# Late expert rows through one-hot products at a layer's end, in a two-layer encoder with a mixture of experts

## Chip, cores and metric

One core of a Trainium2 chip runs the whole program in one launch. The metric is the device time of that launch in microseconds (us), the median of three runs. A profiled execution gives the trace.

## What is computed

Two token groups (256 and 512 tokens, D_MODEL 1024, float32) pass through two layers that share weights between the groups, and a final RMSNorm. Together they are 768 tokens, six tiles of 128. Of the reference only this matters here:

```python
for l in range(DEPTH):                                   # DEPTH = 2
    h = rms_norm(x, norm_mix_g[l])
    x = x + hybrid_mixer(h, ...)                         # four mixers, gates, w_out
    h = rms_norm(x, norm_ffn_g[l])
    x = x + hierarchical_moe(h, ...)                     # 16 experts, top-2 of one group of 4
return rms_norm(x, final_norm_g)

# hierarchical_moe: combine[token, expert] is the weight of a chosen expert, else 0
hid = silu(h @ w1[e]) * (h @ w3[e]) * combine[..., e]
out = sum_e hid_e @ w2[e]
```

## The kernel before

**Stages.** Each layer has a head, a mixer and a tail. The head makes the normed, transposed rows of the six tiles and their first projections. The tail holds the output product, the routing, the experts, and adds what they give to x. After the last layer a short head (layer == L) has the final norm and the stores of the outputs. Each engine runs a program of its own in written order, and semaphores tie them. Between two layers SyncE waits until four engines have raised `layer_over`, clears the layer's semaphores, and raises `cleared`, for which each engine waits in `next_layer` (GpSimd only after its first gathers).

**Experts.** The tokens that chose an expert are scattered into 128-row blocks in DRAM. A block is loaded, transposed on TensorE (`turn_in`), multiplied (`up`), gated, multiplied again (`down`), and its rows leave PSUM through `rows_out`: VectorE copies columns 0 to 511 and ScalarE 512 to 1023 into `y_sb`, and ScalarE issues the store. `ORDER` has the twelve experts whose number is not 3 modulo 4 first; the last of them, at position LOOP = 11, runs in a loop whose count depends on the data. Then come the four late experts 3, 7, 11 and 15, at positions 12 to 15 (END = 15). Early rows go back into `blocks`, late rows into `late_dram`, which has one row of zeros behind its 512 rows.

**Bringing rows back.** `gather` (GpSimd, two indirect DMAs a tile) fetches a token's two rows of `blocks`, and `combine` (VectorE, two operations of 128x1024 a tile) adds them to x with weights. They run beside the late experts: `combine` of tile 0 at position 12, of 2 at 13, of 3 and 4 at 14, of 1 behind the copy of 12, and of 5 behind the copy of 15. What came from a late expert comes by `gather_late`, one indirect DMA a tile through `late_slots`, at the start of the next head, and `add_late` (VectorE, 128x1024) adds it with the weight `w_late`. Since a token's two experts lie in one group, it has at most one late expert. `split_late` (VectorE, behind the copy of position 2) makes `late_slots` and `w_late`; a token with no late row points to the zeros.

**The head.** For tile t: ScalarE squares x (`head_square`), VectorE makes the variance, GpSimd its power -0.5 (`power`), VectorE scales (`scale`), TensorE transposes (`turn`), ScalarE evicts to hT (`evict`). `x_new` counts tiles whose x is complete; SyncE then stores that tile to DRAM. Tiles 0 and 3 are projected plainly (`tile`); tiles 1, 2 and 4, 5 go in pairs through seven smaller products (`pair`), which need sums of weight quarters (`weights_sum`) and of row quarters (`rows_sum`). Before, in layer 1 the four weight sums stand first on VectorE, then add_late(0), tile 0's variance and scale, and add_late(1) and (2). In the last head VectorE has, per tile, variance(t+1), scale(t), add_late(t+3).

**Times of an engine's order.** GpSimd in the head of layer 1 before: gathers of tiles 0 to 4, then power(0), the gather of tile 5, then the other powers. The first gather waits for all four late stores:

```python
if t == 0:
    pool.wait_ge(late_out, 16 * LATE * layer)
    pool.wait_ge(combined, TOP * T * layer)
```

Lines of the profile: L632 gather, L639 combine, L648 gather_late, L844 add_late, L848 and L959 variance and power, L866 scale, L701 the head's transposes, L725 `tile`, L742 `pair`, L873 weights_sum, L882 rows_sum, L2167 turn_in, L2175 up, L2210 down, L2303 the late stores, L2580 VectorE's copy in rows_out, L822 the first of the rope operations.

## Time and profile before

| | us |
|---|---|
| median of three runs | 1974.15 (1974.12 to 1975.18) |
| profiled execution, its own time | 1973.74 |
| its span in the trace | 1971.8 |
| TensorE busy | 1899.3 (96%) |
| VectorE, ScalarE, GpSimd busy | 1134.3, 477.5, 400.4 |
| DMA | 376.32 MB, mean 191 GB/s |

The span runs from the first to the last record of the trace; 1.9 us of the execution's time lie around it. Busy shares are means over stages with quite different limits. Times in rows count from the span's start.

### The profile page before, as it was taken

The numbers are of one execution on the slowest core, as the hardware profiler recorded it, in microseconds if no ns is written. First come the engines' busy times: TensorE is split into PE (matmuls) and PEld (weight loads), VectorE is DVE, ScalarE is ACT, GpSimd is POOL, SyncE is SP. The second block draws the span as 40 slices with busy tenths as digits, with TensorE's granted clock in tenths as the row PEclk, the third lists the DMA queues.
The fourth block names the chain that finished last, engine by engine and source line by source line (L and its number), as shares of the span: only waits on it lengthen the run. The fifth ranks groups of instructions, "written<-read, shape, count | busy, mean of one in ns | idle before, by whom it ended". The sixth has DMA issues, their size and how long they took to land.

```text
span 1971.8 us, 25238 instructions
## 1 busy us (share of the span) xinstructions
PE 1899.3 (96%) x9028; PEld 1251.7 (63%) x9028; DVE 1134.3 (58%) x2171; ACT 477.5 (24%) x1048; POOL 400.4 (20%) x310
## 2 busy tenths in 40 slices
PE   8999999999999999999699999999999999999993
PEld 5655658755665545888565556586566655468882
DVE  4788732644786866111667886436457778641126
ACT  3133313343221011111132333132432300111112
POOL 1322233122220012000324222421222200210013
PEclk9999999999999999999899999999999999999997
DMA  4555677422328405999832121122223392179996
GB/s 178 203 203 203 228 276 270 176 99 79 127 86 322 156 33 217 411 393 369 329 112 113 75 75 75 43 86 81 86 86 118 126 347 91 70 274 424 384 373 235
DMA packets 77915, 376.32 MB, mean 191 GB/s; under 512 B 6705, under 2 KB 15281, under 8 KB 64578
## 3 DMA queue, kind: packets, MB, share of 16 engines
q1 hardware_dynamic: 43154, 260.35, 34.3%
q10 hardware_dynamic: 26000, 82.90, 11.0%
q0 software_dynamic: 8640, 31.46, 4.2%
q8 instruction: 75, 1.23, 0.3%
q14 instruction: 46, 0.38, 0.1%
HBM read 262.44 MB, written 113.30 MB: 191 GB/s over the span
## 4 chain that ended last, share of the span: by engine, by line
PE 89%; DVE 4%; DMA 3%; ACT 1%; issue 1%; POOL 1%; ACTq 0%; DVEq 0%; SPq 0%; POOLq 0%
PE bank L1030 41%; PE bank L2175 11%; PE bank L2035 8%; PE bank L2060 5%; PE bank L2210 5%; PE bank L1043 3%; PE bank L1056 2%; PE bank L1083 2%; PE bank L1121 2%; PE bank L742 2%; PE bank L1095 1%; PE bank L2167 1%; PE bank L1220 1%; PE bank L725 1%; DMA blocks<-ring,slots 1%
## 5 line engine op out<-in xcount | busy, mean ns | idle before, releaser
L1030 PE MATMUL bank<-x,ring 128*128 128x384 f32 x1056 | 360.2, 489 | 2.3 <-issue 2.3
L1030 PE MATMUL bank<-hT,ring 128*128 128x384 f32 x1056 | 359.7, 490 | 0.1
L1030 PEld LDWEIGHTS bank<-x,ring 128*128 128x128 f32 x1056 | 195.0, 190 | 135.2 <-issue 12.5
L1030 PEld LDWEIGHTS bank<-hT,ring 128*128 128x128 f32 x1056 | 195.3, 190 | 133.0 <-issue 10.2
L1525 DVE SCALAR_TENSOR_TENSOR reg_a<-cvx,pp,reg_a 128x783 f32<-128x783 f32 x120 | 142.7, 1189 | 4.3
L1284 ACT ACTIVATE sums<-bank 128x384 f32<-128x384 f32 x132 | 64.9, 491 | 250.0 <-PE bank L1030 243.9
L2571 DVE SCALAR_TENSOR_TENSOR prob<-prob,bank 128x256 f32<-128x256 f32 x30 | 12.6, 421 | 180.8 <-ACT prob L2290 180.7
L1468 DVE SCALAR_TENSOR_TENSOR gbuf<-bank,sums 128x384 f32<-128x384 f32 x96 | 53.5, 557 | 88.0 <-PE bank L1030 82.1
L1805 POOL TENSOR_TENSOR ring<-dg,ring 128x512 f32<-128x512 f32 x24 | 34.1, 1421 | 257.1 <-PE bank L1030 257.1
L2258 ACT ACTIVATE prob<-x 128x1024 f32<-128x1024 f32 x12 | 12.7, 1058 | 291.7 <-DVE x L2423 291.7
L2035 PE MATMUL bank<-oT,wide 128*128 128x384 f32 x256 | 82.9, 486 | 0.0
L2035 PE MATMUL bank<-oT,reg_a 128*128 128x384 f32 x256 | 82.9, 486 | 0.0
L1779 POOL TENSOR_TENSOR ring<-ring 128x512 f32<-128x512 f32 x44 | 60.6, 1378 | 99.0 <-PE bank L1030 76.6
L1298 ACT ACTIVATE gbuf<-gbuf,small 128x384 f32<-128x384 f32 x96 | 59.1, 615 | 74.2 <-DVE gbuf L1468 67.1
L1805 POOL TENSOR_TENSOR ring<-cvx,ring 128x512 f32<-128x512 f32 x20 | 25.4, 1272 | 242.9 <-PE bank L1030 242.9
L2367 POOL TENSOR_TENSOR small<-small 128x1 f32<-128x1 f32 x12 | 6.8, 564 | 315.1 <-DVE small L2428 315.1
L2035 PEld LDWEIGHTS bank<-oT,reg_a 128*128 128x128 f32 x256 | 48.6, 190 | 33.9
L2035 PEld LDWEIGHTS bank<-oT,wide 128*128 128x128 f32 x256 | 48.6, 190 | 33.9
L1030 PE MATMUL bank<-x,dg 128*128 128x384 f32 x192 | 65.9, 486 | 0.0
L2060 PE MATMUL bank<-hT,oT 128*128 128x512 f32 x144 | 65.7, 595 | 0.0
L1333 ACT ACTIVATE probT<-bank 128x256 f32<-128x256 f32 (+2 forms) x96 | 42.9, 446 | 92.2 <-PE bank L1095 89.2
L632 POOL DMA_INDIRECT ring<-blocks,slots x4 | 3.9, 964 | 301.0 <-SPq L2021 300.4
(387 smaller groups left out, 3276.2 us busy)
## 6 DMA issues: line engine op xcount, KB each, us to landing
ring<-in_wd SPq DMA_DIRECT2D x26, 2048.0 KB, 9.2
blocks<-hT SPq DMA_DIRECT2D x16, 3072.0 KB, 22.1
gate_dram<-gbuf ACTq DMA_DIRECT2D x64, 384.0 KB, 2.3
ring<-gate_dram SPq DMA_DIRECT2D x16, 1536.0 KB, 7.3
ring<-in_we SPq DMA_DIRECT2D x8, 2048.0 KB, 15.0
hT<-blocks ACTq DMA_DIRECT2D x26, 512.0 KB, 9.3
wide<-in_we SPq DMA_DIRECT2D x6, 2048.0 KB, 23.1
oT<-in_we SPq DMA_DIRECT2D x6, 2048.0 KB, 21.4
```

Source lines behind the costliest of these rows:

```text
L1030: mm = nc.tensor.matmul(bank[i % 2][:, 0:HALF], w[:, k, :], a[:, k, :], start=(k == 0 and r in (0, 1, 3)), stop=(k == 3), skip_group_check ...
L1043: mm = nc.tensor.matmul(bank[i % 2][:, 0:BW], a[:, k, p * P:(p + 1) * P], w[:, k, :], start=(k == 0 and r in (0, 1, 3)), stop=(k == 3), sk ...
L1284: out(activate(sums[:, r // 2 if r < 3 else 0, :], b, ACT.Copy, scale=scale), i)
L1298: done(activate(c, c, ACT.Tanh, scale=0.5, bias=half(n)), cv_tanh if name == "cv" else None)
L1468: ins = stt(to, b, scale, held_rows, ALU.mult, ALU.add)
L1525: done(stt(y, src, w, y, ALU.mult, ALU.add), last)
L1779: done(tensor_(b12, b12, b11, ALU.subtract), t_done)
L1805: done(tensor_(b11, t2_of(name, g), b11, ALU.subtract), t_done)
L2035: mm = nc.tensor.matmul(branch_bank(q)[:, 0:HALF], wb_sb[m // 4][:, n, k, (m % 4) * P:(m % 4 + 1) * P], oT[:, 2 * n + k, half[hf]], start= ...
L2060: mm = nc.tensor.matmul(bank[out_bank[r]][:, :], a[:, k, p * P:(p + 1) * P], w[:, k, :], start=(k == 0 and r not in (2, 5)), stop=(k == 3) ...
L2175: mm = nc.tensor.matmul(bank[s][:, j * P:(j + 1) * P], up_w[slot][:, k, j * P:(j + 1) * P], xT[s][:, k, :], start=(k == 0), stop=(k == KD ...
L2210: mm = nc.tensor.matmul(y_bank(b)[c][:, :], hidT[s][:, k, :], down_w[slot][:, k, c * 512:(c + 1) * 512], start=(k == 0), stop=(k == 1))
```

## The change

Tiles 0 and 1 (`BY_PRODUCT = 2`) no longer get the rows of the last two late experts (positions 14 and 15) by a gather. `split_late` makes for each of these tiles and each of the two experts a matrix of 128x128 that has, for each token with a row there, w_late at that row's column, and it turns such tokens' `late_slots` to the row of zeros. TensorE transposes the four matrices ahead of down(14), ScalarE evicts them into `sums`, and behind down(15) TensorE multiplies them with the two `y_sb` tiles into PSUM banks 4 to 7 (`end_product`). `add_end` (VectorE, two operations of 128x512 a tile) adds that to x. The gathers of tiles 0 and 1 fetch rows of the first two late experts alone: they are issued in the tail, behind the last `gather`, once those two stores have landed. Their places are now those of tile 2's early rows. combine of tile 5 moves from the tail's end to the next head: in layer 1 behind scale(2), in the last head behind scale(0) and add_end(1). In layer 1's head the weight sums stand behind it, the fourth one behind norm(3), and add_late(3), (4), (5) and the squares of tiles 3 and 4 have new places. TensorE raises `layer_over` behind the first end product. The last 256 rows of `late_dram` are set to zero once, in layer 0. Some semaphores are merged to make room for the new ones.

```diff
-                for t in range(3):
-                    if t == 2:
-                        variance(0)
-                    add_late(t)
-                for t in range(T):
+                combine(dve, L - 1, T - 1)
+                for t in range(1, T):
                     if t + 1 < T:
-                        variance(t + 1)
+                        add_late(t + 1)
+                    variance(t)
                     scale(t)
-                    if t + 3 < T:
-                        add_late(t + 3)
                 return
```

```diff
 def head_vector(dve, layer):
+            def add_end(t):
+                dve.wait_ge(end_mm, BY_PRODUCT * (layer - 1) + t + 1)
+                for c in range(2):
+                    xs = x[:, t, c * 512:(c + 1) * 512]
+                    done(tt(xs, end_bank[t][c][:, :], xs, ALU.add), x_new if c else None)
...
+            if layer:
+                add_late(0)
+                add_end(0)
+                add_late(1)
+                variance(0)
+                scale(0)
+                add_end(1)
...
             if layer:
-                for n in range(4):
-                    weights_sum(n)
-                add_late(0)
-                variance(0)
-                scale(0)
-                add_late(1)
                 add_late(2)
+                norm(1)
+                norm(2)
+                combine(dve, layer - 1, T - 1)
...
+            weights_sum(0)
+            weights_sum(1)
             rows_sum(1, 0)
             rows_sum(1, 1)
+            if layer:
+                add_late(3)
             pair(1, 1)
...
+            weights_sum(2)
+            rows_sum(1, 2)
+            if layer == 0:
+                weights_sum(3)
+            rows_sum(1, 3)
             norm(3)
+            if layer:
+                weights_sum(3)
             pair(1, 4)
             pair(1, 5)
+            if layer:
+                add_late(4)
+                add_late(5)
...
 def head_gpsimd(pool, layer):
-            for t in range(T - 1):
-                gather_late(pool, layer, t)
+            gather_late(pool, layer, 2)
+            gather_late(pool, layer, 3)
             pool.wait_ge(cleared, layer)
             pool.sem_inc(entered, 1)
-            power(0)
-            gather_late(pool, layer, T - 1)
-            for t in range(1, T):
+            for t in range(T):
                 power(t)
+                if t == 0:
+                    gather_late(pool, layer, 4)
+                if t == (1 if layer == L else 2):
+                    gather_late(pool, layer, 5)
...
 def head_scalar(act, layer):
             evict(2)
             head_square(act, layer, 3)
-            head_square(act, layer, 4)
+            if layer == 0:
+                head_square(act, layer, 4)
             for r in (0, 2, 3):
                 pair(1, r)
             evict(3)
             pair(1, 6)
+            if layer:
+                head_square(act, layer, 4)
             head_square(act, layer, 5)
...
 def tail_tensor(pe):
+                    elif b + 1 < NE:
+                        pe.wait_ge(table_done, 3)
+                        for n in range(2 * BY_PRODUCT):
+                            mm = nc.tensor.transpose(bank[2][:, n * P:(n + 1) * P], at_end[n // 2][n % 2], ident)
+                        mm.then_inc(xt_mm, 1)
                     down(b)
+
+                def end_product(t, n):
+                    for c in range(2):
+                        mm = nc.tensor.matmul(end_bank[t][c][:, :], end_rows[t][n], y_sb[n][:, c * 512:(c + 1) * 512],
+                                              start=n == 0, stop=n == 1)
+                    return mm
+
+                pe.wait_ge(xt_ev, pos(END) + 3)
+                pe.wait_ge(y_ev, pos(END))
+                pe.wait_ge(y_ev_act, pos(END))
+                end_product(0, 0)
+                pe.wait_ge(y_ev, pos(END) + 1)
+                pe.wait_ge(y_ev_act, pos(END) + 1)
+                pe.sem_inc(layer_over, 1)
+                end_product(0, 1).then_inc(end_mm, 1)
+                end_product(1, 0)
+                end_product(1, 1).then_inc(end_mm, 1)
...
 def tail_gpsimd(pool):
                     gather(pool, layer, t)
+                for t in range(BY_PRODUCT):
+                    gather_late(pool, layer + 1, t)
...
 def split_late():
+                    for t in range(BY_PRODUCT):
+                        for n in range(2):
+                            done(ts_(at_end[t][n], slot_no, end_slot[:, n, t:t + 1], w_late[:, t:t + 1], ALU.is_equal, ALU.mult),
+                                 table_done if t and n else None)
...
 def tail_vector(dve):
-                    for t in {LOOP + 1: (1,), LOOP + 3: (4,), LOOP + 4: (5,)}.get(b, ()):
+                    for t in {LOOP + 1: (1,), LOOP + 3: (4,)}.get(b, ()):
                         combine(dve, layer, t)
```

## Rows read from the trace of the kernel before

**Rows 1.** The page: busy us, share of the span and instructions of each engine.

```profile
PE 1899.3 (96%) x9028; PEld 1251.7 (63%) x9028; DVE 1134.3 (58%) x2171; ACT 477.5 (24%) x1048; POOL 400.4 (20%) x310
```

**Rows 2.** Windows: stretch, length, busy us of PE, PEld, DVE, ACT, POOL; PEclk, DMA.

```profile
969.20:983.80 14.60, 0.00 (x0) 0.00 (x0) 10.96 (x12) 1.69 (x3) 8.36 (x7) 0.66 0.60 208
...
1943.20:1943.40 0.20, 0.00 (x0) 0.00 (x0) 0.20 (x1) 0.00 (x0) 0.00 (x0) 0.63 0.90 369
```

**Rows 3.** Timeline from layer 0's end: start us, us, instruction [idle before <-releaser].

```profile
965.51 3.60 PE L2210 MATMUL bank<-reg_a,prob 128*128 128x512 f32 x8
...
969.35 0.69 DVE L2580 COPY hT<-bank 128x512 f32<-128x512 f32 x1
...
971.27 1.28 DVE L639 SCALAR_TENSOR_TENSOR x<-gbuf,small,x 128x1024 f32<-128x1024 f32 x1
973.02 1.23 DVE L873 TENSOR_TENSOR wide<-ring 128x1024 f32<-128x1024 f32 x1 [0.46 <-SPq L2642]
973.31 1.74 POOL L648 DMA_INDIRECT reg_b<-late_dram,late_slots  x1 [15.56 <-DMA late_dram<-hT]
...
979.01 1.28 DVE L844 SCALAR_TENSOR_TENSOR x<-reg_b,small,x 128x1024 f32<-128x1024 f32 x1 [0.98 <-DMA reg_b<-late_dram,late_slots]
...
981.58 0.15 DVE L848 TENSOR_SCALAR small<-small 128x1 f32<-128x1 f32 x1 [1.29 <-ACT prob L759]
981.82 0.57 POOL L959 TENSOR_TENSOR small<-small 128x1 f32<-128x1 f32 x1 [0.72 <-DVE small L848]
982.42 1.29 DVE L866 SCALAR_TENSOR_TENSOR reg_a<-x,small,probT 128x1024 f32<-128x1024 f32 x1 [0.69 <-POOL small L959]
...
983.86 1.94 PE L701 MATMUL bank<-consts,reg_a 128*128 128x128 f32 x8 [14.76 <-DVE reg_a L866]
...
986.58 7.55 PE L725 MATMUL bank<-ring,hT 128*128 128x512 f32 x12 [0.78 <-ACT hT L770]
```

**Rows 4.** Timeline of layer 1's head, further on.

```profile
993.96 1.04 PE L701 MATMUL bank<-consts,reg_a 128*128 128x128 f32 x8
...
998.80 0.69 DVE L882 TENSOR_TENSOR x<-hT 128x512 f32<-128x512 f32 x1 [3.85 <-ACT hT L770]
...
1001.41 5.42 PE L742 MATMUL bank<-wide,x 128*128 128x256 f32 x24 [0.36 <-ACT sums L782]
...
1011.81 1.36 DVE L822 TENSOR_TENSOR oT<-reg_b 128x1152 f32<-128x1152 f32 x1 [1.86 <-ACT reg_b L782]
...
1016.95 1.09 PE L701 MATMUL bank<-consts,reg_a 128*128 128x128 f32 x8 [0.65 <-DVE reg_a L866]
```

**Rows 5.** Timeline of the last head.

```profile
1945.18 0.94 POOL L648 DMA_INDIRECT reg_b<-late_dram,late_slots  x1 [14.66 <-DMA late_dram<-hT]
...
1949.82 1.28 DVE L844 SCALAR_TENSOR_TENSOR x<-reg_b,small,x 128x1024 f32<-128x1024 f32 x1 [5.40 <-DMA reg_b<-late_dram,late_slots]
...
1952.75 1.29 DVE L844 SCALAR_TENSOR_TENSOR x<-reg_b,small,x 128x1024 f32<-128x1024 f32 x1 [1.64 <-DMA reg_b<-late_dram,late_slots]
...
1954.31 1.54 POOL L959 TENSOR_TENSOR small<-small 128x1 f32<-128x1 f32 x1 [2.39 <-DVE small L848]
...
1968.71 0.33 SPq L2622 DMA_DIRECT2D y_sample<-hT  x1
```

**Rows 6.** One late store (956.1), one gather (956.8), and their times to landing.

```profile
L2303 ACTq DMA_DIRECT2D late_dram<-hT x1: 333/333/333, 956.1 to 956.1; - x1
...
DMA to landing us min/median/max: 5.3/5.3/5.3
...
L632 POOL DMA_INDIRECT gbuf<-blocks,slots x1: 937/937/937, 956.8 to 956.8; - x1
...
DMA to landing us min/median/max: 11.8/11.8/11.8
```

**Rows 7.** Groups by shape, 1600 to 1740 us; and timeline behind layer 0's split_late.

```profile
L2423 DVE SCALAR_TENSOR_TENSOR x<-bank,x 128x512 f32<-128x512 f32 x26 | 17.9, 690 | 11.3 <-PE bank L2060 10.9
...
835.39 0.42 DVE L2571 SCALAR_TENSOR_TENSOR prob<-prob,bank 128x256 f32<-128x256 f32 x1 [4.34 <-ACT prob L2290]
```

More of the change, by code:

```diff
@@ L116 @@
 FROM_BLOCKS = T - 2
+BY_PRODUCT = 2
 ML_UNITS = [(hp, p) for hp in range(HEADS // 2) for p in range(T // 2)]
@@ L547, in program @@
         setup_done, stored = once("setup_done"), once("stored")
-        late_out, combined = once("late_out"), once("combined")
+        late_out, end_out, end_mm = [once(f"late_out{n}") for n in range(2)], once("end_out"), once("end_mm")
+        combined = once("combined")
         layer_over, cleared, entered = once("layer_over"), once("cleared"), once("entered")
-        x_in, ident_in, consts_done = [once(f"x_in{t}") for t in range(T)], once("ident_in"), once("consts_in")
+        x_in, ident_in = [once(f"x_in{t}") for t in range(T)], once("ident_in")
         first_half, gain_spread = once("first_half"), once("gain_spread")
@@ L624, in y_late @@
         def y_late(t):
-            return reg_b[:, t * D:(t + 1) * D]
+            return reg_b[:, t * D:(t + 1) * D] if t >= BY_PRODUCT else back_place[2][t]
+        end_rows = [[sums[:, :, :].rearrange("p s c -> p (s c)")[:, (2 * t + n) * P:(2 * t + n + 1) * P] for n in range(2)]
+                    for t in range(BY_PRODUCT)]
+        end_bank = [bank[4:6], bank[6:8]]
         def gather(pool, layer, t):
@@ L643, in gather_late @@
         def gather_late(pool, layer, t):
-            if t == 0:
-                pool.wait_ge(late_out, 16 * LATE * layer)
-                pool.wait_ge(combined, TOP * T * layer)
+            if t < BY_PRODUCT:
+                pool.wait_ge(late_out[0], 16 * (2 * layer - 1))
+                pool.wait_ge(combined, TOP * (T * (layer - 1) + 3))
+            else:
+                pool.wait_ge(late_out[0], 32 * layer)
+                pool.wait_ge(end_out, 16 * layer)
+                pool.wait_ge(combined, TOP * (T * (layer - 1) + t + 1))
+            pool.wait_ge(late_out[1], 16 * layer)
             pool.indirect_dma_start(
@@ L768, in evict @@
                 act.wait_ge(ht_mm, t + 1)
+                if layer and t == 0:
+                    act.wait_ge(end_out, 16 * layer)
+                    act.wait_ge(late_out[0], 32 * layer)
                 for q in range(2):
@@ L1854, in mix_sync @@
                 sp.dma_start(late_dram[LATE * P:LATE * P + 1, :], zeros_in[0:1, :]).then_inc(zeros_out, 16)
+                for n in range(LATE - 2, LATE):
+                    sp.dma_start(late_dram[n * P:(n + 1) * P, :], zeros_in).then_inc(zeros_out, 16)
             sp.wait_ge(proj_mm, last_proj[MIX_CHUNKS - 2] + 1)
@@ L1924, in tail @@
             at_late, in_late = (part(752 + 48 * n, T * TOP * LATE).rearrange("p (a g) -> p a g", g=LATE) for n in range(2))
+            end_slot = part(872, 2 * BY_PRODUCT).rearrange("p (n t) -> p n t", n=2)
+            past_two, to_zero = part(880, BY_PRODUCT), part(888, BY_PRODUCT)
+            at_end = [[part((2 * t + n) * P, P) for n in range(2)] for t in range(BY_PRODUCT)]
             w_in, row_late = part(848, T * TOP).rearrange("p (t c) -> p t c", c=TOP), part(864, T)
@@ L1935, in y_free @@
                     eng.wait_ge(loop_over, 1)
-                elif b > LOOP + 2:
-                    eng.wait_ge(late_out, 16 * LATE * layer + 32)
+                elif b == LOOP + 3:
+                    eng.wait_ge(late_out[0], 16 * (2 * layer + 1))
+                elif b == END:
+                    eng.wait_ge(late_out[1], 16 * (layer + 1))
             start_f, expert_f, block_f = part(704, SPARE), part(720, SPARE + 2), part(736, SPARE + 1)
@@ L2302, in rows_out @@
                         n = b - LOOP - 1
-                        act.dma_start(late_dram[n * P:(n + 1) * P, :], y_sb[s]).then_inc(late_out, 16)
+                        act.dma_start(late_dram[n * P:(n + 1) * P, :], y_sb[s]).then_inc(end_out if b == END else late_out[n % 2], 16)
                 turn_in(0)
@@ L2345, in tail_scalar @@
                         turn_in(b + 2)
+                    elif b + 1 < NE:
+                        act.wait_ge(xt_mm, pos(END) + 2)
+                        activate(sums[:, :, :].rearrange("p s c -> p (s c)")[:, 0:4 * P], bank[2][:, :], ACT.Copy).then_inc(xt_ev, 1)
                     rows_out(b)
@@ L2363, in tail_gpsimd @@
                 pool.wait_ge(rows_init, 16 * NE)
-                pool.wait_ge(zeros_out, 16 * (layer + 2))
+                pool.wait_ge(zeros_out, 16 * (layer + 4))
                 for n, t in enumerate(tile_order):
@@ L2566, in split_late @@
                     done(tt(w_both, w_both, w_in, ALU.subtract))
+                    for t in range(BY_PRODUCT):
+                        for n in range(2):
+                            done(ts_(at_end[t][n], slot_no, end_slot[:, n, t:t + 1], w_late[:, t:t + 1], ALU.is_equal, ALU.mult),
+                                 table_done if t and n else None)
                 def hidden(b):
```

52 lines of the change are left out of this document (23 added, 29 removed).

## The prediction

> **What bounds the kernel.** I read the page first: TensorE is busy for 96% of the span [rows 1], so time can only be won where it stands still. The windows show the widest hole: from 969.20 to 983.80 us it does nothing at all [rows 2], and the same place comes once more at the end, after which it has no work left. Both are layer ends. Then I read the timeline across them.
>
> At layer 0's end the last down product starts at 965.51 and ends at 969.11. The rows go to DRAM, and VectorE combines tile 5 until 972.55. The gather of late rows starts on GpSimd at 973.31 and lands 5.6 us after that; VectorE, which had waited for it, adds tile 0 at 979.01 [rows 3]. So x of tile 0 is new at 980.30 (call such a moment X), the square, the power on GpSimd and the scaling follow, and TensorE gets its first transpose at 983.86. The reader is to see a chain of latencies in which each engine waits for the last.
>
> Behind it lies the head of layer 1. TensorE's tile products run on, and its wait ends last on VectorE again at 1016.95, for the scaled rows of tile 4 [rows 4]. From X to there before: 36.65 us. After 1016.95 its waits are of a kind that I take to move along unchanged. The last end is another thing: there the end is set by VectorE and GpSimd, x(0) is new at 1951.10 (1949.82 + 1.28), but VectorE is nearly full from 1952.75 on, and the last store goes at 1968.71, behind the last scaling [rows 5].
>
> **Start of the head, both ends.** Added to TensorE before the last but one down product: four 128x128 transposes. Eight take 1.04 us [rows 4], so 0.5 us, and nothing hides them: down(END) starts at 966.03 and ends at 969.63. ScalarE's extra eviction of 128x512 (0.6 us) falls in the time of the down product. VectorE's copy of the last rows started at 969.35 behind combine(4) and ended at 970.04 [rows 3]; now it ends near 970.36, the store goes 0.3 us later, and the first gather behind it (tile 2 now) starts at 973.64.
>
> The products: one down product is eight instructions of 128x512 in 3.60 us [rows 3], of which each end_product has four, 1.73 us. The first needs only the rows of the expert before the last, and follows at 969.5; the second needs the copy of 970.36, which is there, and runs 971.2 to 973.1. The other two hold TensorE until 976.6, when it has nothing else to do anyway. The clear of semaphores waits for TensorE's release behind the first product (about 971), then 0.47 us as now (972.55 to 973.02 [rows 3]), so add_late(0) of 1.28 us runs from 971.4 to 972.8 and is hidden. Its gather leaves GpSimd when the write of expert LOOP+2 has landed (956.1 + 5.3 = 961.4 [rows 6]), near 962. Then add_end(0): two operations of 128x512 from PSUM, 0.69 us each [rows 7] and 0.04 between: X = 974.53, 5.77 us earlier. All the same at the second end, 971.87 us later by the gathers' starts [rows 3, 5]: X = 1946.40 against 1951.10.
>
> **GpSimd.** power(0) is now queued behind two gathers that wait for the last store: tile 2 from 973.64 to 974.6, tile 3 from 974.9. A gather needs 0.94 us (1945.18 [rows 5]), but one that starts under a VectorE operation with both inputs in SBUF ends about 0.8 us after that operation: the gather of 973.31 took 1.74 us beside the subtraction of 973.02, which lasts 1.23 [rows 3]. add_late(1) runs 974.56 to 975.84, so tile 3's gather ends at 976.68, power(0) starts 0.2 later instead of at 976.05, and the scaling is 0.83 us late. I take that at both ends. The bounds are 0 and 1.3 (one such operation).
>
> The Trainium skill ("SBUF — State Buffer", Who interferes with whom) says that a VectorE operation with two SBUF inputs holds up only GpSimd's reads, and infers that descriptor generation goes free beside a tensor_tensor. The gather just named speaks against the inference. By that rule the 0.83 would fall away twice and the sum below be 1.7 us lower.
>
> **Head of layer 1, from X to the transpose of tile 4.** By VectorE's order: square 1.28, power 0.84, scale 1.29 as in [rows 3] (3.41); transpose at full clock and evictions until the square of tile 1, 2.25; its variance 1.25, power and scale 2.1 (9.0); the same for tile 2, 2.15 (11.2). Then the moved combine(5), 2.6, and two weight sums of 1.26, which before lay in the wait for gathers: 16.3. rows_sum twice, 0.73 each: 17.8. In before VectorE waited 3.85 us ahead of the row sums [rows 4]; that idle swallows most of the addition. add_late(3), 1.3: 19.1. Now the new wait: ScalarE has the square of tile 3 ahead of the eviction of pair(1,0), 1.1, so TensorE's pair(1,2) starts at 20.7 after a stall of some 2.9 us, where before it was 0.36 [rows 4]. VectorE: pair, weight sum, two row sums, variance and scale of tile 3: 26.0; weight sum and pair(1,4): 27.7; pair(1,5), bound by TensorE: 29.3; add_late(4) and (5), 2.6: 31.95; rope piece 0, 3.0 (two operations of 1.36, the first that of 1011.81 [rows 4], and a short one); variance and scale 2.1: 37.05; TensorE 37.1. That is 0.45 longer than the 36.65 of before, from an X that counts 5.77 - 0.83 = 4.94 earlier: a gain of 4.5 us.
>
> **Last head.** From X: scale(0) ends at 4.24 (with the 0.83); add_end(1) 1.45; combine(5) 2.6 that before lay in the wait for the gather: 8.3. Per tile then add_late 1.31, variance, power and scale 2.14. Before, variance(t+1) stood ahead of scale(t), so the power was hidden; now scale(t) stands right behind variance(t) and waits 0.66 of it each time. Four such tiles of 3.45 and a last of 2.15: X + 24.25 = 1970.65. The last store then goes at 1970.7, against 1968.71: a loss of 2.0 us.
>
> **The clock.** The granted clock is at its upper level (2.4 GHz) until the idle of 14.6 us and then at the lower, and the transposes and the first twelve instructions of tile 0 take 1.94 and 7.55 us against 1.04 and 5.2 at full clock (twelve at the pace of the down product's eight) [rows 3, 4]. Now TensorE is idle for only 2.4 us before the first transpose, and 2.9 before pair(1,2). At the last end it fell 2.3 us behind the last product (1940.98 to 1943.3), at layer 0's end after about 4.7 (a mean of 0.66 over 14.6 us between 1.0 and 0.5) [rows 2], so either gap may or may not cost it. Bounds: 0, and 3.2 (0.9 + 2.3, what it costs now). I take 0.7, since VectorE's chain hides the rest.
>
> **Hidden at no cost.** split_late gets six small operations (0.2 us) and four one-hot ones of 128x128 (under 0.35 us each, half of 128x512), 2.6 us on VectorE, which idled 4.34 behind it [rows 7]; uncovered, they would cost 2.6 twice. Two more stores of zeros stand in SP's queue in layer 0, among the mixer's products, where nobody waits for SP. The merged semaphores change no order. SP's x stores and the load of the next chunk move with x(3), from 992.5 to about 995.5; it is used after 1017.
>
> **Sum.** -4.5 + 2.0 + 0.7 = -1.8 us. The profiled execution took 1973.74 (span 1971.8 and 1.9 around it), so 1971.9; the median of the runs is 0.4 higher: 1972.4.
>
> **Rivals.** *Faster*: GpSimd isn't held and the clock stays up: 0.83 twice and 0.7 better, -4.2, 1970.0. For it: the skill's rule, and add_end reads PSUM. Against: the rows of 973.31 and 1954.31, where a power of 0.57 took 1.54 beside VectorE [rows 5]. Chance 0.22. Beyond it lies a head bound by TensorE alone, 1968.
>
> *Slower*: the work put on VectorE is not swallowed in layer 1's head. combine(5) 2.6, four weight sums 5.0 and add_end(1) 1.45 are 9.1 (the 0.45 found above counts them with the idle they fill); if all of it is on the path, the head loses 4.1, and with 2.0 and 0.7 the time is 1981. It decides against the change once less than 2.9 of the 9.1 finds a gap. Against it are the 3.85 and 1.86 us of idle in [rows 4]. Chance 0.1.
>
> *It does not do what it says*: the early gathers land late, since transfers are dense there. A gather issued at 956.8 took 11.8 us [rows 6]. From 962 and 963 that gives 973.8 and 975; X moves to 976.5, of which 1.2 count at the first end: 1973.6. Chance 0.15.
>
> **Numbers.** My forecast has 0.5, and 0.03 lies elsewhere. 0.2% is 3.9 us, about what a measurement can tell from no change. Faster by more than that needs the first rival or luck: 0.25. Slower: 0.12. Between: 0.63. The forecast's own range is 1970.5 to 1974.5; the range that holds 8 in 10 is 1968.0 to 1976.5.
>
> **What would show it.** In the profile after: first transpose of layer 1 near 978.9; a gather of 1.7 us ahead of power(0); TensorE idle 2 to 3 us before pair(1,2), ended by ScalarE; the transpose of tile 4 near 1012.5; in the last head waits of 0.66 us before each scale and the last store near 1967 on the new span's scale. Wrong it would be if the clock stays low for long, or add_late(0) waits for its gather.

## The result, and the profile after

The changed kernel took 1977.92 us (median of 14 runs, 1976.53 to 1982.79) where before took 1975.62 beside it: a ratio of 1.0015, 95% interval 1.0008 to 1.0022. A second set of runs of the same text gave 1978.05 against 1974.98, 1.0017 (1.0008 to 1.0026). So it is slower by 2.3 to 3.1 us by the medians, and by 3.0 and 3.4 by the ratios, which are taken without a few executions of 2036 us and more in the later sets. That is less than the 0.2% named above, but it lies outside the predicted range, and on its other side. The profiled execution took 1980.01 us, with a span of 1978.2.

The timeline of the changed kernel across layer 0's end and the start of layer 1's head answers to [rows 3] (start us, us, instruction, [idle before <-releaser]):

```profile
972.43 7.03 PE L2296 MATMUL bank<-hT,sums 128*128 128x512 f32 x16
...
973.40 0.33 ACTq L2361 DMA_DIRECT2D late_dram<-hT  x1
974.18 1.28 DVE L861 SCALAR_TENSOR_TENSOR x<-dg,small,x 128x1024 f32<-128x1024 f32 x1 [0.81 <-SPq L2716]
976.14 1.42 DVE L868 TENSOR_TENSOR x<-bank,x 128x512 f32<-128x512 f32 x2 [0.67 <-PE bank L2296]
...
977.59 1.28 DVE L861 SCALAR_TENSOR_TENSOR x<-reg_a,small,x 128x1024 f32<-128x1024 f32 x1
977.84 1.84 POOL L659 DMA_INDIRECT reg_b<-late_dram,late_slots  x1 [9.22 <-DMA late_dram<-hT]
...
979.99 0.94 POOL L659 DMA_INDIRECT reg_b<-late_dram,late_slots  x1 [0.30 <-issue]
980.96 0.57 POOL L986 TENSOR_TENSOR small<-small 128x1 f32<-128x1 f32 x1
981.56 1.28 DVE L890 SCALAR_TENSOR_TENSOR reg_a<-x,small,probT 128x1024 f32<-128x1024 f32 x1 [2.50 <-POOL small L986]
...
982.99 1.94 PE L712 MATMUL bank<-consts,reg_a 128*128 128x128 f32 x8 [3.54 <-DVE reg_a L890]
...
985.71 6.87 PE L736 MATMUL bank<-ring,hT 128*128 128x512 f32 x12 [0.78 <-ACT hT L784]
```

The end products do what was wanted: VectorE adds them at 976.14, and x of tile 0 is new at 977.56 with no gather behind the last store. But GpSimd's next gather (tile 2) waits for that store until 977.84, a second one follows, and only then comes power(0): VectorE stands idle for 2.50 us before the scaling, and TensorE for 3.54.

Further on in the same head, to the transpose of tile 4, which answers to [rows 4]:

```profile
996.09 1.09 ACT L784 ACTIVATE hT<-bank 128x512 f32<-128x512 f32 x2 [0.27 <-PE bank L712]
...
997.99 0.69 DVE L906 TENSOR_TENSOR x<-x,hT 128x512 f32<-128x512 f32 x1
998.71 1.28 DVE L861 SCALAR_TENSOR_TENSOR x<-reg_b,small,x 128x1024 f32<-128x1024 f32 x1
1000.03 1.06 ACT L770 ACTIVATE prob<-x 128x1024 f32<-128x1024 f32 x1 [2.86 <-DVE x L861]
...
1001.09 0.36 ACT L796 ACTIVATE sums<-bank 128x256 f32<-128x256 f32 x1
...
1001.60 3.02 PE L753 MATMUL bank<-wide,x 128*128 128x256 f32 x8 [2.09 <-ACT sums L796]
...
1019.64 1.09 PE L712 MATMUL bank<-consts,reg_a 128*128 128x128 f32 x8 [1.46 <-DVE reg_a L890]
```

TensorE stalls for 2.09 us ahead of 1001.60: ScalarE's eviction stands behind the square of tile 3, the square behind add_late(3), and that behind rows_sum. (Among the squares only that of tile 4 has a new place on ScalarE; the square of tile 3 stands where it stood before, and what moved is the addition that it waits for.)

The windows (length, busy us of PE, PEld, DVE, ACT, POOL; PEclk; DMA share; GB/s) show that both idle times cost the clock, as [rows 2] show it for the one of before:

```profile
979.46:982.99 3.53, 0.00 (x0) 0.03 (x1) 1.39 (x2) 0.00 (x0) 3.01 (x4) 0.84 0.69 216
983.00:988.00 5.00, 4.22 (x11) 2.71 (x12) 2.70 (x4) 2.94 (x5) 1.25 (x2) 0.50 0.85 260
999.50:1001.60 2.10, 0.01 (x2) 0.04 (x1) 0.52 (x2) 1.42 (x3) 0.00 (x0) 1.00 0.35 140
...
1003.00:1005.00 2.00, 2.00 (x6) 1.55 (x6) 1.80 (x4) 0.29 (x1) 0.01 (x1) 0.50 0.92 328
```

0.50 is the lower level (1.2 GHz), 1.00 the upper.

The last head, which answers to [rows 5] (two of the five tiles behind tile 0, and the last scaling):

```profile
1949.25 1.79 POOL L659 DMA_INDIRECT reg_b<-late_dram,late_slots  x1 [7.96 <-DMA late_dram<-hT]
...
1952.91 1.28 DVE L890 SCALAR_TENSOR_TENSOR hT<-x,small,probT 128x1024 f32<-128x1024 f32 x1 [2.50 <-POOL small L986]
...
1961.80 1.28 DVE L861 SCALAR_TENSOR_TENSOR x<-reg_b,small,x 128x1024 f32<-128x1024 f32 x1
...
1963.12 0.15 DVE L872 TENSOR_SCALAR small<-small 128x1 f32<-128x1 f32 x1
1963.36 0.56 POOL L986 TENSOR_TENSOR small<-small 128x1 f32<-128x1 f32 x1 [0.74 <-DVE small L872]
1963.95 1.28 DVE L890 SCALAR_TENSOR_TENSOR hT<-x,small,probT 128x1024 f32<-128x1024 f32 x1 [0.68 <-POOL small L986]
...
1967.41 1.28 DVE L890 SCALAR_TENSOR_TENSOR hT<-x,small,probT 128x1024 f32<-128x1024 f32 x1 [0.66 <-POOL small L986]
...
1973.00 1.29 DVE L890 SCALAR_TENSOR_TENSOR hT<-x,small,probT 128x1024 f32<-128x1024 f32 x1 [0.66 <-POOL small L986]
```

A tile takes 3.46 us (1963.95 to 1967.41), of which 0.66 is the wait for the power.

**The span added up.** From the end of each layer's last up product (before: 961.96 and 1933.83, after: 965.01 and 1936.36), the two spans, 1971.8 and 1978.2, divide like this: up to layer 0's end +3.0; from there to the transpose of tile 4 54.99 before and 54.63 after, -0.4; the body of layer 1 -0.2; from its last up product to the last store 34.88 and 37.95, +3.1; from that store to the end of the span 3.1 and 3.9, +0.8. Together +6.4 with rounding. The first +3.0 can't be called the change's: in the eleven further profiles below, all with the change's operations in layer 0, that point lies anywhere from 961.7 to 964.4, on average 0.7 behind the one profile of before, and a0_again, the same text, has it at 963.1. So some tenths of a us in layer 0 may be the change's; one profile of before can't tell. What is left, +3.3, is the cost at the two layer ends and behind them in this execution.

### The profile page after: what moved, and what is told of

Same layout as the page of the kernel before. It is cut to its first block, busy times and chain, and to the rows that moved or that the text cites. A ratio compares the mean times of both kernels' runs of the same rounds, so it can differ in the third digit from the quotient of the medians.

```text
span 1978.2 us, 25377 instructions
## 1 busy us (share of the span) xinstructions
PE 1915.3 (97%) x9068; PEld 1259.2 (64%) x9068; DVE 1144.6 (58%) x2199; ACT 478.9 (24%) x1050; POOL 399.6 (20%) x310
## 3 DMA queue, kind: packets, MB, share of 16 engines
q8 instruction: 75, 1.23, 0.2%
## 4 chain that ended last, share of the span: by engine, by line
PE 89%; DVE 4%; issue 2%; DMA 2%; POOL 1%; ACT 1%; ACTq 0%; POOLq 0%; DVEq 0%; SPq 0%
PE bank L1059 41%; PE bank L2211 10%; PE bank L2071 8%; PE bank L2096 5%; PE bank L2246 5%; PE bank L1072 3%; PE bank L1085 2%; PE bank L1112 2%; PE bank L1150 2%; PE bank L753 2%; PE bank L1124 1%; PE bank L2203 1%; PE bank L1249 1%; PE bank L736 1%; DMA blocks<-ring,slots 1%
```

## The experiments

All are compared by two stretches. A is the start of the last but one down product, which follows the four added transposes (some 0.45 us per layer end, so not in the stretches). The head stretch runs from A in layer 0 to the first transpose of tile 4; the end stretch from A in layer 1 to the end of the span. Between the two lies the body of layer 1, which is in neither: 917.3 us in the changed kernel, and from 916.8 to 921.7 in the others, so a difference of spans or of single times can't be put down to the two stretches alone. One execution each, and each ratio is to runs of before made beside that kernel's; the columns between say when scale(0) started in layer 1's head (from A), how long TensorE had stood idle before the first transpose and before pair(1,2), and whether the clock fell there.

| kernel | scale(0) | idle, first transpose | idle, pair(1,2) | head stretch | end stretch | ratio to before (95%) |
|---|---|---|---|---|---|---|
| before | 20.35 | 14.76, fell | 0.36 | 54.88 | 37.86 | 1 |
| changed | 16.00 | 3.54, fell | 2.09, fell | 54.08 | 41.29 | 1.0015 (1.0008 to 1.0022) |
| a0_again | 14.76 | 2.29, fell | 2.09, stayed | 51.86 | 41.32 | 1.0017 (1.0008 to 1.0026) |
| e1_power_first | 14.19 | 1.73, stayed | 4.47, fell | 54.30 | 41.17 | 1.0016 (1.0007 to 1.0025) |
| e4_pe_busy | 16.01 | 0.96, stayed | 1.23, stayed | 51.04 | 41.26 | 1.0012 (1.0003 to 1.0021) |
| e5_no_early_gathers | 14.77 | 2.30, stayed | 2.96, fell | 51.17 | 39.71 | 1.0010 (1.0002 to 1.0019) |
| e2_combine_tail | 16.29 | 3.83, fell | 2.09, fell | 54.62 | 38.66 | 1.0005 (0.9996 to 1.0014) |
| e3_var_early | 18.10 | 5.64, fell | 2.09, fell | 56.82 | 38.98 | 1.0003 (0.9994 to 1.0012) |
| e6_square3_later | 16.34 | 3.87, fell | none, stayed | 52.04 | 41.52 | 0.9994 (0.9985 to 1.0003) |
| e8_first_end_only | 16.00 | 3.54, fell | 2.09, stayed | 53.11 | 37.53 | 0.9993 (0.9984 to 1.0002) |
| e9_first_end_add3 | 17.54 | 5.07, fell | none, stayed | 53.04 | 37.72 | 0.9977 (0.9967 to 0.9988) |
| e10_both_new_order | 15.73 | 3.26, fell | none, stayed | 50.84 | 34.71 | 0.9972 (0.9960 to 0.9983) |
| e12_new_order_pe_busy | 16.30 | 1.26, stayed | none, stayed | 48.49 | 35.56 | 0.9969 (0.9956 to 0.9981) |

**a0_again: the changed kernel once more.**

> The changed kernel once more, beside the others, as their yardstick. Two stretches are read in each trace: the head stretch, from the end of layer 0's last up product to the first transpose of layer 1's tile 4 (before 54.99 us, changed 54.63), and the end stretch, from the end of layer 1's last up product to the issue of the last store (before 34.88, changed 37.95). All theories: 54.6 and 38.0 again, within 1 us.

The same text gave a head stretch 2.2 us shorter, where no more than 1 us of difference was expected. Its second moved gather had landed, at 971.4, when the last late store was issued at 971.5, and the store took 2.6 us; in the first profile that gather landed at 975.0, 1.6 us behind the store's issue, and the store took 3.7. So the gather of tile 2 could start at A + 11.21, where the first profile had 12.28, and it took 0.94 us and not 1.84; scale(0) came 1.24 us earlier and the clock fell once, not twice. The last end is the same to 0.03; there the gather of tile 2 started at A + 12.55. So one profile's head stretch of this kernel can't be read to better than 2 us unless it is said what the clock and the store did in it.

**e1_power_first: power(0) ahead of the two gathers.**

```
             pool.wait_ge(cleared, layer)
             pool.sem_inc(entered, 1)
             for t in range(T):
                 power(t)
                 if t == 0:
+                    gather_late(pool, layer, 2)
+                    gather_late(pool, layer, 3)
                     gather_late(pool, layer, 4)
```

> GpSimd takes power(0) of tile 0 ahead of the gathers of tiles 2 and 3. Theory Q (the late last store and the two gathers queued ahead of power(0) hold up the scaling of tile 0 by 1.9 us at both ends): the scaling starts 2.1 us after x of tile 0 is new instead of 4.0, head stretch 1 to 2 us shorter, end stretch 1.9 shorter, time 2 to 4 us less. Rival V (VectorE's longer list decides whatever GpSimd does, and gathers issued later make add_late(2) wait): under 1 us in each stretch.

The two gathers are taken out ahead of it. The scaling came 1.8 us earlier and the first clock loss was gone, but nothing was won: the gather of tile 2 now left at A + 14.36, add_late(2) waited 3.37 us for it, scale(1) came at 22.44 as in the changed kernel (22.46), and the stall before pair(1,2) grew to 4.47 us and took the clock there. At the last end it went the same way: scale(0) at 14.20, add_late(2) 1.79 us in wait, scale(1) at 23.52 for 23.57. The wait moved from power(0) to the gather, and the 2 to 4 us of the theory didn't come; the rival was right.

**e4_pe_busy: TensorE kept busy in both gaps** by products of 128x512 that nobody reads.

```
                 end_product(1, 1).then_inc(end_mm, 1)
+                if layer == 0:
+                    for n in range(3):
+                        nc.tensor.matmul(bank[3][:, :], end_rows[0][0], y_sb[0][:, 0:512], start=True, stop=True)
...
+                if layer and t == 1 and r == 2:
+                    for n in range(2):
+                        nc.tensor.matmul(bank[5][:, :], hT[:, 0, 0:P], w[:, 0, :], start=True, stop=True)
```

> TensorE gets idle work whose result nobody reads: three 128x512 products into a free bank behind layer 0's end products, and two ahead of pair(1,2), sized to lie inside the idle of 3.5 and 2.1 us. Theory C (the idle lets the granted clock fall twice, and that costs up to 3 us of the head stretch): clock at its upper level throughout, first transposes 1.04 us instead of 1.94, the 24 instructions of pair(1,2) to (1,4) 5.4 instead of 7.1, head stretch 1.5 to 3 us shorter, end stretch unchanged. Rival V (VectorE decides): clock up, head stretch the same within 0.5 us.

This is the clean measurement of the clock: scale(0) stands at 16.01, the first transpose at A + 17.44, as in the changed kernel's profile (16.00, 17.43), and the head stretch is 3.04 us shorter: pair(1,2) started 1.50 us earlier (34.54 for 36.04 from A) and took 1.7 less. The times show less of it: 1.0012 against 1.0015 and 1.0017, with intervals that overlap. In this execution the body of layer 1 took 919.25 us against 917.27, and no run says why. The windows of this kernel show the clock at its upper level in the gap, through the transposes and ahead of pair(1,2):

```profile
976.50:979.50 3.00, 3.00 (x8) 1.14 (x6) 0.46 (x3) 0.03 (x1) 2.52 (x4) 1.00 0.65 224
980.80:982.60 1.80, 1.05 (x8) 0.82 (x8) 1.73 (x3) 0.71 (x2) 0.70 (x1) 1.00 0.72 234
996.50:998.50 2.00, 0.77 (x4) 0.59 (x4) 0.59 (x2) 1.25 (x3) 0.00 (x0) 1.00 0.70 250
```

**e5_no_early_gathers: without the moved gathers of tiles 0 and 1.** The rows that they bring are missing, so x of tiles 0 and 1 lacks the earlier late experts.

```
-            dve.wait_ge(gathered[t], 16 * ((TOP + 1) * layer + TOP))
+            dve.wait_ge(gathered[t], 16 * ((TOP + (t >= BY_PRODUCT)) * layer + TOP))
...
-                dve.wait_ge(gathered[t], 16 * (TOP + 1) * layer)
+                if t >= BY_PRODUCT:
+                    dve.wait_ge(gathered[t], 16 * (TOP + 1) * layer)
...
-                for t in range(BY_PRODUCT):
-                    gather_late(pool, layer + 1, t)
```

> The two gathers of late rows for tiles 0 and 1 are left out, at both layer ends (add_late(0) and (1) still run, on what lies there). Theory D (these two transfers, now issued beside the last two late stores, make the last one land 1.2 us later): the last late store lands in 2.6 us instead of 3.7, the gather of tile 2 and power(0) come 1.1 us sooner, each stretch about 1 us shorter. Rival: the store is late because TensorE and VectorE are busy with its rows, so 3.7 us again and no gain.

The last store landed undelayed at both ends (the gather of tile 2 at A + 11.21 and 11.22; before had 11.24 at both), scale(0) stood at 14.77 at both, and the end stretch was 1.6 us shorter. Its timeline:

```profile
974.04 0.94 POOL L659 DMA_INDIRECT reg_b<-late_dram,late_slots  x1 [14.43 <-DMA late_dram<-hT]
...
975.28 1.69 POOL L659 DMA_INDIRECT reg_b<-late_dram,late_slots  x1 [0.30 <-issue]
...
976.98 0.58 POOL L987 TENSOR_TENSOR small<-small 128x1 f32<-128x1 f32 x1
977.60 1.28 DVE L891 SCALAR_TENSOR_TENSOR reg_a<-x,small,probT 128x1024 f32<-128x1024 f32 x1 [1.26 <-POOL small L987]
```

VectorE's wait for the power is 1.26 here, 2.50 in the changed kernel. The moved gathers thus cost about 1.2 us at an end where they are still on their way when the last store is issued; at a0_again's first end they weren't, and scale(0) stood at 14.76 with them. The head stretch is 2.9 us shorter than the changed kernel's, not 1, since the first clock loss went too: TensorE was idle for 2.30 us and kept its level.

**e2_combine_tail: combine(5) back behind the last copy.**

```
-                combine(dve, L - 1, T - 1)
...
-                combine(dve, layer - 1, T - 1)
...
-                    for t in {LOOP + 1: (1,), LOOP + 3: (4,)}.get(b, ()):
+                    for t in {LOOP + 1: (1,), LOOP + 3: (4,), LOOP + 4: (5,)}.get(b, ()):
```

> Combine(5) goes back to its place behind the copy of the last rows, at both layer ends; the one-hot products stay. Head stretch: start of the last but one down product of layer 0 to the first transpose of tile 4 (before 54.9 us, the changed kernel 54.1 in one execution, 51.9 and 51.0 to 54.3 in others). End stretch: the same start in layer 1 to the end of the span (before 37.9, changed 41.3). Theory (VectorE's order decides): x of tile 0 comes about 1.2 us later, behind the combine, but VectorE's chain behind it is 2.6 us shorter, so the stall of 2.1 us ahead of pair(1,2) goes, the clock doesn't fall there, head stretch 51.5, end stretch 39.9; time about 3 us below the changed kernel. Rival (what counts is only how early x of tile 0 is): both stretches 1.2 us longer than in the changed kernel.

x of tile 0 came 1.53 us later at both ends. At the last end the theory held, and more: scale(1) 2.6 us earlier (20.96 for 23.57), an end stretch of 38.66 for the 39.9 expected. scale(0) stayed where it was (16.04 for 16.00). In the changed kernel it waited for gathers; here they were done in time, since the store had landed early (A + 11.20), and the later x set it: the two came out alike by chance. In layer 1's head the theory fell: the stall stayed at 2.09 us. VectorE now had time to spare:

```profile
997.03 0.69 DVE L906 TENSOR_TENSOR x<-hT 128x512 f32<-128x512 f32 x1 [3.54 <-ACT hT L784]
997.75 0.69 DVE L906 TENSOR_TENSOR x<-x,hT 128x512 f32<-128x512 f32 x1
998.48 1.28 DVE L861 SCALAR_TENSOR_TENSOR x<-reg_b,small,x 128x1024 f32<-128x1024 f32 x1
...
1001.36 1.92 PE L753 MATMUL bank<-wide,x 128*128 128x256 f32 x6 [2.09 <-ACT sums L796]
```

It is not the amount of work on VectorE but the order: rows_sum waits for the eviction of tile 2, and add_late(3), which needs nothing of it, stands behind.

**e6_square3_later: the square of tile 3 behind the eviction of pair(1,0).**

```
-            head_square(act, layer, 3)
             if layer == 0:
+                head_square(act, layer, 3)
                 head_square(act, layer, 4)
             for r in (0, 2, 3):
                 pair(1, r)
+                if layer and r == 0:
+                    head_square(act, layer, 3)
```

> Only on ScalarE, head of layer 1: the square of tile 3 goes behind the eviction of pair(1,0), instead of ahead of it. Theory (the square, which waits for add_late(3) behind combine(5), holds the eviction, and so TensorE before pair(1,2), which also costs the clock): stall of 2.1 us before pair(1,2) gone or under 0.5, pair(1,2) of 24 instructions 5.4 us instead of 7.1, head stretch 50 to 51.5 us. Rival (VectorE is the bound of that head anyway): the stall goes, but tile 4's first transpose stays where it is and waits longer for VectorE, head stretch 51.5 to 54. End stretch 41.3 by both.

The stall went, and the clock stayed up there: pair(1,2) took 5.3 us. The head stretch is 2.04 us shorter than the changed kernel's with a scale(0) 0.3 later. At 52.04 it is 0.5 above what was expected, since the clock still fell behind the first gap (tile(0) took 8.46 us). That lies in the rival's range, but the rival's mechanism isn't seen: the transpose of tile 4 moved with it and waits 1.46 us for VectorE, as in the changed kernel. The median is 1.1 us below before's, where the changed kernel's were 2.3 and 3.1 above; no stretch shows more than 2.0 of these 3.4 to 4.2 us.

**e3_var_early: in the last head the variance ahead of the next tile's addition.**

```
+                    variance(t)
                     if t + 1 < T:
                         add_late(t + 1)
-                    variance(t)
                     scale(t)
```

> Only in the last head: the variance of tile t is taken before the late rows of tile t+1 are added, so that GpSimd's power lies under that addition. Theory (exposed power of 0.66 us a tile is what made the last head longer): no wait of 0.66 us before the scalings of tiles 1 to 4, each tile 2.8 in place of 3.46 us, end stretch 41.3 - 2.6 = 38.7 us, head stretch as in the changed kernel. Rival (the last head is bound by the gathers, which land late): the 0.66 turn into waits for gathers, end stretch stays over 40.5.

The waits shrank only from 0.66 to 0.51 us, and a tile from 3.46 to 3.18 (22.05, 25.3, 28.47, 31.65 from A): the power of 0.55 us takes 1.52 beside the addition. Half of the 2.3 won comes from scale(0) instead (14.77 for 16.00), because the last store landed early in this execution; the edit itself brought 1.1 us of the 2.6 expected.

```profile
1964.11 1.27 DVE L861 SCALAR_TENSOR_TENSOR x<-reg_b,small,x 128x1024 f32<-128x1024 f32 x1
1964.27 1.52 POOL L986 TENSOR_TENSOR small<-small 128x1 f32<-128x1 f32 x1 [1.65 <-DVE small L872]
...
1965.89 1.28 DVE L890 SCALAR_TENSOR_TENSOR hT<-x,small,probT 128x1024 f32<-128x1024 f32 x1 [0.51 <-POOL small L986]
```

At this execution's first end the moved gathers left late (A + 2.97 and 4.69, after the second late store had landed at 964.8, A + 2.2) and add_late(0) waited for one of them:

```profile
973.97 1.28 DVE L861 SCALAR_TENSOR_TENSOR x<-dg,small,x 128x1024 f32<-128x1024 f32 x1 [3.54 <-DMA dg<-late_dram,late_slots]
```

x of tile 0 was 2.1 us later and the head stretch 56.8, longer than before's: the rival of the late landing, seen in one layer end of this kernel's two.

**e8_first_end_only: the change at layer 0's end alone**, with before's last end.

```
-            if layer == L:
-                combine(dve, L - 1, T - 1)
-                for t in range(1, T):
...
+            if layer == L:
+                for t in range(3):
+                    if t == 2:
+                        variance(0)
+                    add_late(t)
...
+                if layer + 1 < L:
                     end_product(0, 1).then_inc(end_mm, 1)
```

> The change at layer 0's end alone: at layer 1's end the rows of tiles 0 and 1 come by gathers and tile 5 is combined as in the kernel before, with its order of the last head. Theory (the change wins at the first end and loses at the last): head stretch as in the changed kernel, 51.9 to 54.3, end stretch as before, 37.9; time 1 to 3 us below before, and 3.4 us below the changed kernel. Rival (the loss is not at the last end but in the body of the layers, by the one-hot operations and the zero stores): end stretch 37.9, yet time not below before.

The end stretch is before's (37.53), the head stretch 53.11, the median 1.6 us below before's and the ratio 0.9993: level with before or just under it. Put back at the last end alone, before's order and gathers take 3.8 us off the end stretch: more than the changed kernel loses lies there, and its head gains too little to pay for it.

**e9, e10, e12: a new order.** The three share, against the changed kernel, combine(5) as in e2 and:

```
                 norm(2)
-                combine(dve, layer - 1, T - 1)
+                add_late(3)
...
-            if layer:
-                add_late(3)
             pair(1, 1)
```

e9 has before's last end; e10 has the products there too, this order in the last head, and the gather of tile 5 ahead of power(1) there; e12 is e10 with the three unread products of e4 at layer 0's end.

```
-                for t in range(1, T):
-                    if t + 1 < T:
-                        add_late(t + 1)
-                    variance(t)
-                    scale(t)
+                add_late(2)
+                variance(1)
+                add_late(3)
+                for t in range(1, T):
+                    if t + 1 < T:
+                        variance(t + 1)
+                    scale(t)
+                    if t + 3 < T:
+                        add_late(t + 3)
```

> The change at layer 0's end alone (last end as in the kernel before), combine(5) at both ends behind the copy of the last rows, and in layer 1's head add_late(3) ahead of the weight sums. Theory (the stall of 2.1 us before pair(1,2) comes from the chain rows_sum, add_late(3), square of tile 3, eviction, and costs the clock a second time; VectorE stood idle for 3.5 us ahead of rows_sum once combine(5) was out of the way, so add_late(3) fits there): no stall before pair(1,2), clock at its upper level from there on, head stretch 51 to 52.5 us (54.6 with combine(5) moved alone), end stretch 37.5 as in the kernel with the first end alone; time about 1 us below that kernel's, 3 below before. Rival (pair(1,2) then waits for something else, such as the eviction's place in ScalarE's queue): a stall over 1 us stays, head stretch over 53.5.

> One-hot products at both ends, combine(5) behind the copy of the last rows, add_late(3) ahead of the weight sums, and in the last head the order of the kernel before: variance of tile t+1, scaling of tile t, add_late(t+3), with the gather of tile 5 ahead of power(1). Theory (the last head was lost by the exposed powers and by combine(5) behind x of tile 0, not by the products): scalings of tiles 1 to 5 from 21.5 us behind the start of the last but one down product, 2.7 apart, end stretch about 34.5 us (before 37.9, changed 41.3), head stretch 51 to 52.5; time 5 to 6 us below before. Rival (the gathers of tiles 3 to 5, which can't start before the late store has landed, are the bound): VectorE waits for them, end stretch 36.5 to 38, time 2 to 3 us below before.

> As the kernel with both ends and the new order, and at layer 0's end three products of 128x512 more that nobody reads, behind the end products, so that TensorE stands idle for about 1 us less 0.6 before the first transpose instead of 3.5. Theory (the clock that falls in the idle is on the path): granted clock 1.00 throughout the head, tile(0) 5.4 us, head stretch 49.5 to 51 us, about 1.5 below the kernel without these products. Rival (VectorE's chain is the bound behind tile 0, so the clock there costs nothing): clock 1.00, yet the head stretch the same within 0.5. End stretch the same by both.

In all three the stall before pair(1,2) is gone. The head stretches are 53.04, 50.84 and 48.49; 51 to 52.5, the same, and 49.5 to 51 were expected. e9 lies above, mainly since its store landed late and scale(0) stood at 17.54. e9 took 1971.40 us, e10 1969.63, e12 1969.50, against 1974.93 for before: 3.5, 5.3 and 5.4 us less. The end stretch of e10 was 34.71 (34.5 expected), its scalings 2.70 us apart, the two shown here with no wait ahead of them:

```profile
1955.03 1.27 DVE L890 SCALAR_TENSOR_TENSOR hT<-x,small,probT 128x1024 f32<-128x1024 f32 x1
1955.19 1.52 POOL L987 TENSOR_TENSOR small<-small 128x1 f32<-128x1 f32 x1 [2.39 <-DVE small L872]
...
1957.73 1.27 DVE L890 SCALAR_TENSOR_TENSOR hT<-x,small,probT 128x1024 f32<-128x1024 f32 x1
```

e12's head stretch of 48.49 is the shortest, 2.35 less than e10's, with a scale(0) 0.57 later: with the clock kept, the first twelve products of tile 0 took 5.39 us for 8.15. The medians of e10 and e12 don't show these 2.35 us, though (7 and 6 runs, intervals of 2 us to each side). In e12's profile the body of layer 1 took 921.66 us, 4.4 more than in e10's, with one wait of 2.64 us for the load of a block at 1746.81, and its end stretch was 0.85 longer. So it is left open how often e10 loses its clock, and whether what the clock gives in the head lasts to the end.

The intervals of all three lie below 1, so they are faster than before, by 0.2 to 0.3%. No run has the new order without the products. At the last end before has this order already, and e10's end stretch is 3.15 us shorter (34.71 for 37.86); in the head the share of the products isn't separated.

## Why the prediction was wrong, point by point

- **X, both ends: right.** x of tile 0 came 5.79 us earlier from the end of the last up product (predicted 5.77), and 4.72 at the last end (4.70). The end products, the early clear and the cover for add_late(0) went as worked out.
- **GpSimd's 0.83: the mechanism right, the term too small.** The gather of tile 2 took 1.84 us beside add_late(1) and ended 0.81 behind it. But the step before it, "the first gather behind it (tile 2 now) starts at 973.64", took the landing of the last late store from before, where nothing else was on its way. In the changed kernel the DMA engines are still busy with a moved gather (landed at 975.0) and the store before it (975.9) when the last store is issued at 973.40; the last store landed 3.7 us after its issue instead of 2.6, and scale(0) started 4.00 behind X in place of the predicted 2.95 (2.12 and the 0.83): 1.05 more, at both ends of this profile, though at the last end alone in a0_again. e5, without the moved gathers, has it back (14.77 from A; the prediction's 977.48 is 14.9).
- **The head's sum without the clock: right.** From X to the transpose of tile 4 it says 37.1 + 0.83. e4, with the clock kept, took 39.04, which is 37.93 and the 1.05 just named, with 0.06 left.
- **The clock's 0.7: the term that failed first.** It was taken near its lower bound "since VectorE's chain hides the rest". e4 gives 3.04 us with all else in its place; the bound was 3.2. In a0_again, where the clock fell once and scale(0) stood 1.25 earlier, the same comparison gives 2.07, an estimate that shifts e4's head by these 1.25. VectorE's chain hides only a part. In the first gap TensorE lost 2.35 us up to the transposes of tile 1 (26.86 for 24.51 from A), and pair(1,2) came 1.50 later: 0.85 was hidden, because VectorE's links from scale(1) on wait for TensorE's transposes and ScalarE's evictions (in e2 VectorE stood idle 3.54 us for those of tile 2). The second loss, 1.5, wasn't hidden at all.
- **The stall before pair(1,2): found in the prediction** (2.9 us, ended by ScalarE; it was 2.09), but it counted as part of a chain in which VectorE is bound, and combine(5) as a cause of it. e2 and e6 show that it comes from add_late(3) behind rows_sum and the square ahead of the eviction alone.
- **The last head: the exposed power right** (four times 0.66), and the last scaling at X + 25.4 for 24.25, which is the 1.05 again. Not foreseen: from the last store to the end of the span it took 3.9 us and not 3.1. It goes with the order of the last head and not with the products: 3.0 to 3.1 in all five kernels with before's order there (before, e8 to e12, two of them with products), 3.5 to 3.9 in the seven without it. How the order does it wasn't isolated.
- **The sum.** -1.8, +1.05 and +0.8 at the last end, +1.05 and +2.35 (3.04 less 0.7) in the head: +3.45, against +3.3 read off this profile. The other execution, a0_again, had 2.2 of it less in the head. The medians, +2.3 and +3.1, lie between the two. So the step that failed is the pricing of three terms: the clock at 0.7 for 2.07 to 3.04 us, the last store's landing taken from before (1.05 at an end), and nothing for the 0.8 behind the last store.
- **The rivals.** GpSimd was held, so the faster one fell: the gather that started under add_late(1) took 1.84 and 1.79 us. The Trainium skill's inference ("SBUF — State Buffer", Who interferes with whom), that descriptor generation goes free beside a tensor_tensor, is spoken against by the gather of [rows 3], which started under a tensor_tensor; these two started under a scalar_tensor_tensor, which has two SBUF inputs as well and held them by as much. The slower one had the direction of the time, but its mechanism didn't act: e4's head agrees with a sum in which all but 0.45 of the 9.1 us of VectorE's work is swallowed. The late landing came true in one layer end of e3.

## What to carry to other kernels

Work moved off the end of a chain takes its transfers along: gathers that leave earlier meet the last store of the old chain, and whatever is queued on GpSimd behind that store waits for both. Where an addition needs nothing of the instruction ahead of it, put it in front: the 1.3 us of add_late(3) in the wrong place cost a stall of 2.1 us and, at times, the clock. Keep the power and the variance one tile ahead of the scaling in a head that VectorE bounds. The products stand in both the kernel of +3 us and that of -5; what differs between these two is the order around them.

## What the runs showed of the hardware

- **Short idle times of TensorE cost the clock, not always.** Ahead of the first transpose of layer 1: idle of 0.96, 1.26 and 1.73 us kept the upper level; of 2.29 it fell, of 2.30 it stayed (another kernel); from 3.26 on it fell each time. Ahead of pair(1,2) a stall of 2.09 us, in five executions, cost it in three. Once fallen, it stayed there for some 3 to 10 us in the kernels with end products (0.50 in the windows), and the transposes and twelve products took up to 1.94 and 8.46 us for 1.04 and 5.39.
- **A power of 0.55 us on GpSimd takes 1.52 beside a VectorE addition with both inputs in SBUF**, so hiding it there wins 0.15 of 0.66 us unless the next instruction of VectorE doesn't need it.
- **A gather is held by where it starts.** Under add_end, which reads PSUM, it took 0.94 us (a0_again, A + 11.21); started ahead of add_late(1) and running on under it, 0.94 too (e10, A + 13.37, the addition from 13.56 on); started under add_late(1), it ended 0.81 behind that (the changed kernel) or 0.82 (e12).
- **The moved gathers scatter the landing of the last store.** Without them the gather that waits for it started at A + 11.2 at all four ends (before, e5), and at A + 11.4 at the last ends of e8 and e9; with them anywhere from 11.2 to 14.5, the latest where they had left last (A + 2.97 and 4.69).
